# Twelve experts held instead of ten: weights loaded under the output projection, three residual tiles in DRAM, and the down projection moved behind the next gate and up

## The reference, cut to what matters

```python
t = modulated rows                                   # 640 x 1024
combine = per token: top-1 group of 4, then top-2 of its 8 experts, two weights    # 640 x 32
hid = silu(t @ w_gate[e]) * (t @ w_up[e])            # 1024 -> 128, for each of 32 experts
out = sum over e of combine[:, e] * (hid @ w_down[e])   # 128 -> 1024
x = layer_norm(ALPHA * x + gate * out)
```

## Time and profile before

| | us |
|---|---|
| median of 3 runs (1308.15 to 1311.05) | 1308.36 |
| profiled execution, its own time | 1308.29 |
| its span, first to last instruction | 1306.4 |
| PE busy in the span | 1190.0 (91%) |
| DVE busy | 590.4 (45%) |
| ACT busy | 350.1 (27%) |
| POOL busy | 186.5 (14%) |
| bytes moved by DMA | 263.5 MB, mean 202 GB/s |

### The profile page before, as it was taken

The page is one execution under the profiler, slowest core; times in us unless marked ns, Lnnn a source line. Parts: engine busy times, 40 slices in busy tenths (PEclk is TensorE's granted clock), DMA queues, the critical chain, the costliest instruction groups (busy, mean ns, idle before and its releaser), DMA issues.

```text
span 1306.4 us, 17530 instructions
## 1 busy us (share of the span) xinstructions
PE 1190.0 (91%) x6771; PEld 690.7 (53%) x6771; DVE 590.4 (45%) x1171; ACT 350.1 (27%) x693; POOL 186.5 (14%) x177
## 2 busy tenths in 40 slices
PE   4999999999999989999998788999999998997784
PEld 2554455545446677455564445655554555664441
DVE  2222332310236666857232116089986855322118
ACT  1334444411315444211221115220033121221122
POOL 1000000010000001130333110800000311351210
PEclk9999999999999999998999999999999999999988
DMA  9513558865010207406999958121115028999953
GB/s 349 201 63 137 191 199 295 281 212 186 15 65 9 69 9 273 176 33 263 364 408 405 395 189 343 44 83 43 63 65 209 33 105 337 408 411 403 363 218 154
DMA packets 97938, 263.50 MB, mean 202 GB/s; under 512 B 12619, under 2 KB 14962, under 8 KB 96962
## 3 DMA queue, kind: packets, MB, share of 16 engines
q1 hardware_dynamic: 81904, 228.26, 46.3%
q0 software_dynamic: 15632, 34.02, 7.1%
q10 hardware_dynamic: 322, 0.12, 0.0%
HBM read 254.53 MB, written 28.79 MB: 217 GB/s over the span
## 4 chain that ended last, share of the span: by engine, by line
PE 72%; SPq 10%; DMA 7%; DVE 6%; ACT 3%; issue 3%; ACTq 0%; DVEq 0%; POOLq 0%
PE ps L2216 17%; PE ps L2227 14%; PE ps L2728 5%; DMA scratch<-in_moe_w_up 4%; SPq L697 3%; SPq L699 3%; PE ps L2106 3%; PE ps L2368 3%; PE ps L2531 2%; PE ps L2745 2%; SPq L696 2%; PE ps L2677 2%; DMA mix_cm<-in_mod_w 2%; PE ps L2512 2%; PE ps L2335 2%
## 5 line engine op out<-in xcount | busy, mean ns | idle before, releaser
L2216 PE MATMUL ps<-h_cm,weights 128*128 128x512 f32 (+1 forms) x832 | 226.8, 434 | 0.0
L2216 PEld LDWEIGHTS ps<-h_cm,weights 128*128 128x128 f32 x832 | 126.3, 191 | 104.0 <-issue 103.7
L2227 PE MATMUL ps<-weights,mix_cm 128*128 128x512 f32 x256 | 112.2, 595 | 0.0
L1719 DVE SCALAR_TENSOR_TENSOR scratch<-scratch,taps_cm 128x655 f32<-128x655 f32 x120 | 101.5, 897 | 2.5 <-ACT scratch L1289 1.0
L2227 PEld LDWEIGHTS ps<-weights,mix_cm 128*128 128x128 f32 x256 | 47.9, 190 | 56.5 <-issue 56.4
L2011 DVE TENSOR_TENSOR scratch<-ps,scratch 128x128 f32<-128x128 f32 x38 | 11.1, 291 | 145.8 <-ACT scratch L1329 145.8
L2728 PE MATMUL ps<-weights,scratch 128*64 128x256 f32 x544 | 64.0, 388 | 12.7 <-DMA weights<-in_moe_w_up 8.7
L2227 PE MATMUL ps<-weights,h_cm 128*128 128x512 f32 (+1 forms) x208 | 71.4, 502 | 0.0
L2728 PE MATMUL ps<-h_cm,scratch 128*64 128x256 f32 x240 | 56.2, 389 | 11.0 <-DMA scratch<-in_moe_w_up 8.2
L2728 PEld LDWEIGHTS ps<-weights,scratch 128*64 128x64 f32 x544 | 43.9, 140 | 34.9 <-issue 12.3
L1392 DVE COPY mod_parts<-ps 128x512 f32<-128x512 f32 x24 | 16.6, 690 | 93.5 <-PE ps L2106 93.5
(11 more groups left out here) (437 smaller groups left out, 2044.4 us busy)
## 6 DMA issues: line engine op xcount, KB each, us to landing
weights<-in_mod_w SPq DMA_DIRECT2D x13, 2048.0 KB, 8.9
x_tm<-in_mod_w SPq DMA_DIRECT2D x10, 2048.0 KB, 8.6
weights<-in_moe_w_gate SPq DMA_DIRECT2D x34, 512.0 KB, 8.4
weights<-in_moe_w_up SPq DMA_DIRECT2D x34, 512.0 KB, 10.6
weights<-in_moe_w_down SPq DMA_DIRECT2D x34, 512.0 KB, 11.1
weights<-in_ab_w_in SPq DMA_DIRECT2D x5, 2048.0 KB, 12.8
weights<-in_cd_w_in SPq DMA_DIRECT2D x5, 2048.0 KB, 15.9
scratch<-in_moe_w_down SPq DMA_DIRECT2D x18, 512.0 KB, 11.5
```

The costliest lines, as they stand in the source:

```text
L1719: ins = V.scalar_tensor_tensor(out=CO[:, j, 0:655], in0=UP[:, j, k:k + 655], scalar=CW[:, 4 * k + j:4 * k + j + 1], in1=CO[:, j, 0:655], o ...
L2216: ins = T.matmul(ps(*name)[:, a:b], w[:, k, col:col + 128], HT[:, k, a:b], start=(k == 0), stop=(k == KD - 1))
L2227: ins = T.matmul(ps(*name)[:, at:at + w.shape[2]], src[:, k, t * 128:t * 128 + 128], w[:, k, :], start=(k == 0), stop=(k == KD - 1))
```

## The change

- The ring holds 12 experts (six pairs), loaded one by one by `load_main(e)`. New places are the first three tiles of X (expert 0), the norm rows LNR (expert 11), scratch that held the gathered rows (expert 4) and one new buffer FREE_DOWN. The gathered rows XG move to other scratch and to GR; small tables of the routing move from OT into the buffer MR.
- To free X, POOL stores residual tiles 0, 1 and 2 to DRAM (XD) as soon as they are scaled, and reads them back after the extra pairs, ahead of moe_done. The scaling of tile 3 now follows at once in the loop over tiles, that of tile 4 stands behind the four first gathers, ahead of the loop over pairs.
- During the output projection SP loads experts 1, 2, 3, the down blocks of 4 and 5, then gate and up of 4 (once the first tile's expert rows are made), then expert 0 (once the three tiles are stored). The rest of 5, experts 6, 7, 8 and gate and up of 9 follow when the last "y" is done; 10, the down blocks of 9 and 11 when the routing products are done; gate and up of 11 when residual tile 4 is scaled.
- In the loop over the 16 pairs PE's order becomes gate_up(u), turn(u+1), down(u-1), turn_hidden(u), and ACT, DVE and POOL follow suit. The extra pairs keep their old order, but use the places of pairs 10 and 11, and the down blocks of an extra pair wait for a later step than before in the second quad.
- In the combine stage of layer 0 tiles 3 and 4 are summed by ACT (weight times the first list, in place) and DVE (one more scalar_tensor_tensor), not by PE; the order of PE's work is written anew. Several semaphores are merged.

```diff
-RING = 5
+RING = 12
+PAIRS_IN_RING = RING // 2
+SPILLED = 3
...
-COMBINE_ORDER = [[("slot", 1), ("gate", 0), ("gate", 1), ("slot", 0), ("ys", 0), ("slot", 3), ("ys", 1), ("ys", 2), ("xT", 0), ("slot", 3), ("ys", 3), ("slot", 1), ("xT", 1),
-                  ("cd", 0, 0), ("slot", 0), ("ys", 4), ("xT", 2), ("cd", 0, 1), ("slot", 3), ("cd", 1, 0), ("cd", 1, 1),
-                  ("slot", 1), ("xT", 3), ("cd", 0, 2), ("cd", 1, 2), ("slot", 0), ("xT", 4), ("cd", 0, 3), ("cd", 1, 3),
-                  ("cd", 0, 4), ("cd", 1, 4), ("slot", 1)],
+PE_MIXED = 3
+COMBINE_ORDER = [[("slot", 1), ("gate", 0), ("gate", 1), ("slot", 0), ("ys", 0), ("slot", 3), ("ys", 1), ("ys", 2), ("xT", 0), ("slot", 0), ("xT", 1),
+                  ("slot", 2), ("cd", 0, 0), ("cd", 1, 0), ("slot", 1), ("xT", 2), ("cd", 0, 1), ("cd", 1, 1),
+                  ("slot", 0), ("xT", 3), ("cd", 0, 2), ("cd", 1, 2), ("slot", 1), ("xT", 4), ("cd", 0, 3), ("cd", 1, 3),
+                  ("cd", 0, 4), ("cd", 1, 4), ("slot", 0)],
                  [("slot", 0), ("gate", 0), ("gate", 1), ("norm", 0), ("norm", 1)] + [("ys", t) for t in range(NT)]]
...
-        EXPERT_AT = [[(W, 0), (W, 3072)], [(W, 6144), (W, 9216)],
-                     [(HTF, 0), (Z, 4096)], [(HTF, 3072), (OTF, 0)], [(OTF, 3072), (GR, 0)]]
-        DOWN_AT = {(2, 1): C[:, COFF["cos"][0]:COFF["cos"][0] + 1024], (3, 0): z(2048, 1024), (4, 0): z(3072, 1024), (4, 1): z(9216, 1024)}
...
+        EXPERT_AT = [(XF, 0), (W, 9216), (HTF, 0), (Z, 4096), (Z, 10240), (W, 6144), (W, 0), (W, 3072),
+                     (OTF, 0), (OTF, 3072), (HTF, 3072), (LNF, 0)]
+        DOWN_AT = {3: C[:, COFF["cos"][0]:COFF["cos"][0] + 1024], 4: FREE_DOWN[:, :], 9: z(3072, 1024), 10: z(2048, 1024), 11: z(9216, 1024)}
+        FIRST_EXTRA = 20
...
+        def rows_moved(l, back):
+
+            return 32 + 16 * SPILLED * (2 * l + 1 + back)
...
-                def load_main(u, i, parts=(0, 1)):
-                    load_expert(l, 2 * u + i, u % RING, i, pair_gu[u % RING], pair_down[u % RING], parts)
-
-                load_main(1, 1)
-                load_main(2, 0)
-                load_main(2, 1)
+                def load_main(e, parts=(0, 1)):
+                    p = e // 2 % PAIRS_IN_RING
+                    load_expert(l, e, e, pair_gu[p], pair_down[p], parts)
+
+                for e in (1, 2, 3):
+                    load_main(e)
+                load_main(4, (1,))
+                load_main(5, (1,))
+                sp.wait_ge(h_ready, 5 * l + 1)
+                load_main(4, (0,))
+                sp.wait_ge(d_xr, rows_moved(l, 0))
+                load_main(0)
                 retire(("wo", l, 1))
-                for u in range(NP0):
-                    if u == 3:
-
-                        filled(sp, "lg", l, 4)
-                        sp.wait_ge(h_ready, 5 * l + 5)
-                    if u == 4:
-
-                        sp.wait_ge(rt_ready, l + 1)
-                        sp.wait_ge(rows_ready, 2 * l + 2)
-                        sp.wait_ge(d_hst[0], 16 * 3 * (l + 1))
-                        sp.wait_ge(d_hst[1], 16 * 2 * (l + 1))
-                    for part, read in enumerate((m["gu"], m["down"])):
-                        at_least(sp, read, u - RING + 1)
-                        for i in range(2):
-                            if (u, i) not in ((1, 1), (2, 0), (2, 1)):
-                                load_main(u, i, (part,))
-
+                load_main(5, (0,))
+                load_main(6)
+                load_main(7)
+                load_main(8)
+                load_main(9, (0,))
+                filled(sp, "lg", l, 4)
+                sp.wait_ge(h_ready, 5 * l + 5)
+                load_main(10)
+                load_main(9, (1,))
+                sp.wait_ge(d_hst[1], 16 * 2 * (l + 1))
+                load_main(11, (1,))
+                sp.wait_ge(x_ready, 10 * l + 5)
+                load_main(11, (0,))
+                for u in range(PAIRS_IN_RING, NP0):
+
+                    sp.wait_ge(m["gu"], u - PAIRS_IN_RING + 1)
+                    for i in range(2):
+                        load_main(2 * u + i, (0,))
+                    for v in ((u - 1, u) if u == NP0 - 1 else (u - 1,)):
+                        if v >= PAIRS_IN_RING:
+                            sp.wait_ge(m["down"], v - PAIRS_IN_RING + 1)
+                            for i in range(2):
+                                load_main(2 * v + i, (1,))
+
+                sp.wait_ge(rt_ready, l + 1)
...
-                                sp.wait_ge(m["x_slot"], j * 4 + (2 * p + part + 1))
+                                sp.wait_ge(m["x_slot"], j * 4 + (1, 3, 3, 4)[2 * p + part])
                                 for i in range(2):
-                                    load_expert(l, pair[i], 1 + p, i, m[f"xw{p}"], m[f"xwd{p}"], (part,))
+                                    load_expert(l, pair[i], FIRST_EXTRA + 2 * p + i, m[f"xw{p}"], m[f"xwd{p}"], (part,))
...
-                    if t < 3:
+                    if t < 4:
                         residual_rows(t)
+                    if t < SPILLED:
+                        pool.wait_ge(x_ready, 10 * l + t + 1)
+                        pool.dma_start(XD[128 * t:128 * t + 128, :], X[:, t, :]).then_inc(d_xr, 16)
...
                 pool.wait_ge(rows_ready, 2 * l + 1)
-                for u in range(4):
+                for u in range(2):
                     gather(u, TIY[:, 0, u:u + 1])
                 pool.wait_ge(rows_ready, 2 * l + 2)
+                for u in range(2, 4):
+                    gather(u, TIY[:, 0, u:u + 1])
+                residual_rows(4)
                 pool.wait_ge(d_mod, MOD_DMAS * 2)
+                def scatter_main(u):
+                    pool.wait_ge(m["ya"], u + 1)
+                    pool.wait_ge(m["yv"], u + 1)
+                    at_least(pool, m[f"s{u % 2}"], 16 * (u // 2))
+                    scatter(u % 2, TIY[:, 1, u:u + 1])
+
                 for u in range(NP0):
-                    par = u % 2
-                    if u in (6, 8):
-                        residual_rows(u // 2)
                     pool.wait_ge(m["t"], u + 1)
                     pool.wait_ge(g_sems[u % 4], (64 * l if u % 4 > 1 else 0) + 16 * (u // 4 + 1))
                     if u < NP0 - 2:
                         gather(u % 4, TIY[:, 0, u + 4:u + 5])
-
-                    pool.wait_ge(m["ya"], u + 1)
-                    pool.wait_ge(m["yv"], u + 1)
-                    at_least(pool, m[f"s{par}"], 16 * (u // 2))
-                    scatter(par, TIY[:, 1, u:u + 1])
-                pool.dma_start(GATE_ROW, MODD[l, 3:4].rearrange("i g c -> i (g c)")).then_inc(d_r5, 16)
+                    if u:
+                        scatter_main(u - 1)
+                scatter_main(NP0 - 1)
...
+                pool.wait_ge(m["down"], (FIRST_EXTRA + 4) // 2 + 1)
+                for t in range(SPILLED):
+                    pool.dma_start(X[:, t, :], XD[128 * t:128 * t + 128, :]).then_inc(d_xr, 16)
...
+                    def weighted_rows(t):
+
+                        act.wait_ge(pair_diag, 2 * NT)
+                        act.wait_ge(d_y[t], 32)
+                        A_(YB[0][:, t, :], YB[0][:, t, :], ACT.Identity, scale=W12[:, 0, t:t + 1]).then_inc(rows_weighted, 1)
...
+                        if t + PE_MIXED < NT:
+                            weighted_rows(t + PE_MIXED)
...
+                        if behind:
+                            if u + 1 < count:
+                                turned(n0, u + 1)
+                            if u:
+                                second_half(n0, s0, u - 1)
 
                         dve.wait_ge(m["ht"], n0 + (u + 1))
                         at_least(dve, m["down"], n0 + (u - 1))
                         V.tensor_copy(HIDT[:, u % 2, :], pair_bank(u)[:, 256:384]).then_inc(m["hc"], 1)
...
+                    if t == 0:
+                        dve.wait_ge(d_xr, rows_moved(l, 1))
+                    if l == 0 and t >= PE_MIXED:
+                        dve.wait_ge(rows_weighted, t - PE_MIXED + 1)
+                        chain(V.scalar_tensor_tensor(out=ZT[:, b, :], in0=YB[1][:, t, :], scalar=W12[:, 1, t:t + 1], in1=YB[0][:, t, :],
+                                                     op0=ALU.mult, op1=ALU.add))
+                        chain(V.tensor_tensor(ZT[:, b, :], ZT[:, b, :], R5[:, g, :], ALU.mult))
...
-                def slot_of_main(u):
-                    return u % RING
+                def main_down(u):
+                    pe.wait_ge(pair_down[u % PAIRS_IN_RING], 32 * uses(u, l))
+                    down(0, u, 2 * u)
 
                 main_turn(0)
                 for u in range(NP0):
-                    p = u % RING
-                    pe.wait_ge(pair_gu[p], 64 * (uses(p, l) + u // RING + 1))
-                    gate_up(0, u, slot_of_main)
+                    pe.wait_ge(pair_gu[u % PAIRS_IN_RING], 64 * uses(u, l))
+                    gate_up(0, u, 2 * u)
                     if u + 1 < NP0:
```

(47 more changed lines are left out.)

96 lines of the change are left out of this document (47 added, 49 removed).

## The result

The changed kernel takes 1298.11 us (median of 4 runs, 1296.91 to 1300.3) against 1309.26 us before (4 runs): ratio 0.9912, 95% interval 0.9897 to 0.9926, so 9.7 to 13.5 us faster. The prediction was 1296.1 us, range 1289.0 to 1303.5. The profiled execution took 1300.3 us, its span is 1298.4 us. It is the longest of the four, and its first load of an expert is issued 2.05 us later than before (525.09, not 523.04), ahead of anything that was changed; times of layer 0 are compared with that taken off.

A forecast was written before the change was run, and what follows sets the result against it. The weights' DMA stream, full at 405 GB/s, was taken to bound the pairs. Gains of 7.4 us in layer 0 and 4.8 in layer 1, together 12.2, took 1308.3 to 1296.1 us, range 1289.0 to 1303.5.

The forecast's parts named there:

- head start: Pairs, both layers: twelve experts issued by gate_up(0)'s end, not ten; gain 7.0 us each, bounds 4.0 to 9.2 and 8.5.
- combine: Combine stage of layer 0: two tiles' sums taken off PE gain 2.0 us, bounds 0 and 7.0.
- The stream is the bound: Pairs: the full DMA stream at 405 GB/s sets the pace; their end moves by the bytes in place earlier.
- standstill: Just before gate_up(0) ends: with the ring full, a stretch of some 5 us with little DMA.
- start-up: Refill at the end of gate_up(0): restarting the DMA stream after it stands still loses 1.5 us.
- PE's order: Pairs: down(u-1) fills PE's waits, a pair costs PE about 6.5 us, hidden behind the DMA stream: 0.
- Tiles to DRAM and back: Before the combine stage: reads back make first lists about 2 us later; cost 1.2 and 1.8 us, bounds 0 and 3.9.
- Tile 3 at once: Scaling beside DVE's residual add and expert choice: POOL delays DVE, net cost 0.4 us a layer, bounds 0 and 2.5.
- rival 3: Tile 3's scaling: the exclusive port lock costs 2.5 us a layer, not 0.4; 1300.3 us, chance 0.08.
- Rival 1: Pairs and combine stage: no restart loss and PE's 7.0 us count in full; gain 20.9 us, 1287.4, chance 0.12.
- Rival 2: Pairs start 2 to 3 us later each layer, reads back cost the full 3.9 us each; 1306, chance 0.14.
- Rival 4: Pairs: waits of 2.9 us before gate_up bring PE's clock down and it stays low; about 1339, chance 0.06.

The follow-up runs named there:

- second profile: The changed kernel itself measured and profiled once more, nothing changed: 1297.52 us, ratio 0.9900 to the kernel before.
- d1_late: The changed kernel with twelve places, but only three experts loaded under the output projection, the others when its weights are released: 1302.55 us, ratio 0.9933.
- c4_tile3: The kernel before with one part of the change, POOL scaling residual tile 3 at once and not at pair 6: 1310.65 us, ratio 1.0007.
- c2_filler1: The changed kernel with residual tiles read back from SP's queue, plus three unused matmuls on PE before layer 1's norm rows' broadcast: 1294.81 us.
- a2_ten: The changed kernel with experts 10 and 11 loaded only once gate_up(0) has ended: 1309.79 us, ratio 0.9997.
- a1_old_order: The changed kernel with the old order of a pair on every engine, down(u) behind turn_hidden(u): 1299.16 us, ratio 0.9912.
- a4_pe_sums: The changed kernel with PE summing all five tiles in layer 0 in that stage's old order: 1303.67 us, ratio 0.9946.

## Why the prediction was right, point by point

The mechanism held. That the sum came out within 2 us of the measured time is partly luck: the terms for the change (head start, combine) and the one against it (reads back) were all too small, and nearly cancelled.

- **The stream is the bound, twelve places are the gain.** Right: with ten experts in place 1309.8 us. The head start was put at 7.0 us less 0.4 in each layer. The stretch to the lists shortens by 8.3 and 8.4 us (8.4 and 9.0 in the second profile), gate_up(0) of layer 0 starts 0.6 to 0.8 us later: 7.5 to 7.7 us in layer 0, and 8.9 to 9.8 in layer 1, where the start was 0 to 1.4 us earlier. In layer 1 that is beyond the bound of 8.5. The standstill was forecast at 5 us and is 7.7 us' worth (133 and 56 GB/s of 408 over ten us), and it isn't the pure loss that the 1.5 us for "start-up" made of it: it serves the gathers, and `d1_late` shows what they cost in a full stream.
- **PE's order 0.** Right in the total (0 to 2 us; alone it gains nothing). The step was not: 6.5 us were forecast, and it is 6.82. The first gate_up that waits for weights is that of pair 14; before the change it was pair 11, and PE and the stream now end nearly together. Waits of 2.9 us after that: 3.98 and 2.22 in layer 0, 1.95, 0.25, 1.64 and 2.52 in layer 1.
- **Tiles to DRAM and back, -1.2 and -1.8.** The term that was mis-sized: 4.5 to 6.3 and 3.8 to 4.1 us in the two profiles of the changed kernel. "The data begin some 1.5 us before the lists do" was of little help: only 32 GB/s moved from 760 to 770, so that the first lists landed 3.0 to 3.4 us later instead of 2. The filler hid none of it: in these two profiles it ran at full clock, ended 4.5 to 4.9 us too early, and PE's first sum then ran at half clock. In the three profiles in which that sum ran at full clock the cost in layer 0 was 2.9 to 3.4 us. The bound of 3.9 us counted the bytes and left out PE's clock. The note "wrong if the first lists come 4 us later" was nearly met.
- **Tile 3 at once, -0.4 a layer.** 0.0 in the rows of `c4_tile3`, layer 0; rival 3 (2.5 us a layer) is out.
- **Combine, +2.0.** 2.7 us against the kernel before, and 4.2 to 4.4 against the three other profiles of the old stage: more than DVE's path alone gives, probably because PE's projections also start earlier (argued).
- **Rival 1** (the gain is larger): not met. The head start passed its 8.5 us in layer 1 but not its 9.2 in layer 0, and the sums off PE gave 2.7 to 4.4 of its 7.0.
- **Rival 2** (most given back): its second mechanism, the full price of the reads back and more, came true, its first (late pairs) only in `d1_late`. **Rival 4:** the clock did fall in gate_up after the waits (0.83 from 720 to 740), in three gate_ups in all (6.07, 5.31 and 5.36 us, not 3.67), but the next one was at full speed each time.

Sum from the second profile: 8.4 - 4.5 + 2.7 in layer 0, 9.0 - 4.1 in layer 1, less 0.5 at the start of gate_up(0): 11.0 us from the rounded columns. Its span is 10.8 us shorter; the forecast was 12.2.

## What to carry to other kernels

When a stream is the bound, count what is in place when its consumer starts, not when it was loaded, and leave a gap in it for small transfers that the consumer waits for first. A spilled buffer's way back belongs behind the last weights in the same queue, where the DMA engines idle, and not beside the first transfer of the next stage. Price a delay of PE with what its clock does afterwards: here 3 us of late data in layer 0 became 4.5 to 6.3 where the clock fell, and stayed 2.9 to 3.4 where it did not.

## What the runs showed of the hardware

- PE's clock fell while PE worked without a gap. In `c2_filler1` it was 0.77 and 0.55 (1250 to 1260) in the broadcasts, matmuls that use one row of the array, and in the sum behind them; the filler between the broadcasts, matmuls of 128 rows, ran at full clock (six in 2.84 us). Yet filler of 128 rows can meet the low clock too. In `c4_tile3`, layer 0, it followed on the broadcasts at 776.7 without a gap, the clock was 0.50 (the stretch below), and its ten matmuls took 6.94 us, not 4.56. What brings the clock down there was not isolated.
- After PE's wait for the first lists of layer 0 its clock was down or not. After waits of 4.5 and 4.9 us (the changed kernel) the first four matmuls of the sum took 3.46 and 3.75 us, after 1.5, 2.7 and 3.3 us (`a2_ten`, `a1_old_order`, `d1_late`) 1.95 us, after 3.2 us (`a4_pe_sums`) 2.59 us.
- An indirect gather took 7.5 us from issue to PE's start on it with the stream at 407 GB/s, and 7.05 us at 405 GB/s (`d1_late`). It took 5.2 us where the stream fell from 403 to 132 GB/s 2.5 us after the issue. In the kernel before (100 and then 253 GB/s) it had landed after 3.4 us.

```profile
775.00:780.00 5.00, 5.00 (x7) 1.69 (x6) 0.00 (x0) 1.16 (x2) 0.00 (x0) 0.50 0.57 182
```
